# Hybrid retention/convolution/MoE step: late constants, an early root for norm 1, and the first four in-projection blocks taken unit by unit

## The reference, cut to what matters

```python
cond = jax.nn.silu(c)
for l in range(2):
    mod = (cond @ w_mod[l] + b_mod[l])[:, None, :]
    sh1, sc1, gt1, sh2, sc2, gt2 = jnp.split(mod, 6, axis=-1)
    h = rms_norm(x, g_mix_norm[l]) * (1 + sc1) + sh1          # norm 1
    proj = h @ w_in[l]                                        # in-projection, 1024 -> 3072
    q, k, v, g, u, z = split(proj)
    a = u * jax.nn.sigmoid(z)                                 # input of the convolution
    cv, buf_new = causal_depthwise_conv(a, conv_buf[l], w_conv[l], b_conv[l])   # 31 taps
    conv_out = jax.nn.silu(layer_norm(cv, g_conv_ln[l], b_conv_ln[l]))
    ret_out, s_new = retention(rotary(q), rotary(k), v, ...)  # gated by silu(g)
    x = x + gt1 * (concat(ret_out, conv_out) @ w_out[l])
    h = rms_norm(x, g_ffn_norm[l]) * (1 + sc2) + sh2
    x = x + gt2 * grouped_moe(h, ...)                         # 16 experts, 2 per token
return rms_norm(x, g_final), states
```

## Time and profile before

| | |
|---|---|
| median of three runs | 1478.28 us (1475.58 to 1479.06) |
| profiled execution | 1475.93 us, of which the span is 1473.4 us |
| PE busy | 1387.0 us, 94% of the span |
| DVE busy | 671.1 us, 46% |
| ACT busy | 240.4 us, 16% |
| DMA, mean | 341 GB/s |
| chain that ended last | PE 63%, SP's queue 25%, DMA 5%, DVE 3% |

### The profile page before, as it was taken

One profiled execution on the slowest core, in us unless ns is written; L12 is line 12 of the kernel. 1 busy time (PEld: TensorE's weight loads), 2 busy tenths in 40 slices (PEclk: granted clock), 3 DMA queues, 4 the chain that ended last, 5 costly groups with the idle time before them and its releaser, 6 DMA issues.

```text
span 1473.4 us, 20499 instructions
## 1 busy us (share of the span) xinstructions
PE 1387.0 (94%) x7451; PEld 657.1 (45%) x7452; DVE 671.1 (46%) x1955; ACT 240.4 (16%) x398; POOL 93.0 (6%) x143
## 2 busy tenths in 40 slices
PE   5899998999999999999989999889999999999996
PEld 2677663433433333343337766543343333334333
DVE  1598655334333333433326967653343323233343
ACT  1211312111110111111121113311111101111112
POOL 1072010000000000000000710000000000000000
PEclk9799997999999999999999999989999999999999
DMA  9934679999999983999998446799999999899993
GB/s 333 370 115 146 236 263 348 406 410 409 410 410 410 409 310 159 391 410 410 410 409 314 180 144 237 267 374 410 410 409 410 409 410 410 335 389 410 410 409 122
DMA packets 131315, 502.10 MB, mean 341 GB/s; under 512 B 8636, under 2 KB 8956, under 8 KB 131139
## 3 DMA queue, kind: packets, MB, share of 16 engines
q1 hardware_dynamic: 127056, 487.84, 83.8%
q0 software_dynamic: 3600, 11.21, 2.7%
q10 hardware_dynamic: 626, 2.62, 0.6%
HBM read 495.48 MB, written 7.00 MB: 341 GB/s over the span
## 4 chain that ended last, share of the span: by engine, by line
PE 63%; SPq 25%; DMA 5%; DVE 3%; issue 2%; ACT 1%; PEldq 0%; PEld 0%; DVEq 0%; ACTq 0%
PE ps L399 59%; SPq L367 22%; PE ps L402 4%; DMA ring<-in_w_mod 3%; DMA ring<-in_w_exp_up 2%; SPq L379 1%; SPq L322 1%; ACT arena L857 1%; DVE stat L1049 1%; ACT L857 0%; SPq L370 0%; DVE rt L1317 0%; ACT stat L857 0%; SPq L366 0%; SPq L313 0%
## 5 line engine op out<-in xcount | busy, mean ns | idle before, releaser
L399 PE MATMUL ps<-ring,arena 128*64 128x512 f32 x3360 | 755.7, 598 | 21.2 <-DMA ring<-in_w_exp_up 15.2
L399 PEld LDWEIGHTS ps<-ring,arena 128*64 128x64 f32 x3360 | 227.7, 137 | 488.4 <-issue 419.0
L399 PE MATMUL ps<-hT,ring 128*128 128x288 f32 x1024 | 257.9, 413 | 11.9 <-DVE hT L1119 9.6
L857 ACT ACTIVATE arena<-ps 128x512 f32<-128x512 f32 (+3 forms) x238 | 127.7, 551 | 832.5 <-PE ps L399 726.0
L1407 DVE SCALAR_TENSOR_TENSOR xT<-ps,mod,xT 128x256 f32<-128x256 f32 x280 | 132.8, 474 | 256.0 <-PE ps L399 256.0
L399 PEld LDWEIGHTS ps<-hT,ring 128*128 128x128 f32 x1024 | 196.7, 193 | 72.2 <-DVE hT L1119 10.1
L399 PE MATMUL ps<-arena 64*128 64x288 f32 (+4 forms) x1656 | 208.4, 404 | 4.5 <-DVE xT L1460 1.7
L399 PEld LDWEIGHTS ps<-arena 64*128 64x128 f32 (+4 forms) x1656 | 117.6, 159 | 128.5 <-issue 100.0
L1150 DVE SCALAR_TENSOR_TENSOR arena<-arena,wcT 128x256 f32<-128x256 f32 x240 | 123.5, 576 | 1.6
L857 ACT ACT_TABLE_LOAD x49 | 62.9, 1283 | 304.2 <-PE ps L399 300.5
L1441 DVE TENSOR_TENSOR arena<-ps,arena 128x512 f32<-128x512 f32 x35 | 24.2, 691 | 166.7 <-PE ps L399 166.7
(11 more groups left out here) (169 smaller groups left out, 528.0 us busy)
## 6 DMA issues: line engine op xcount, KB each, us to landing
ring<-in_w_exp_gate SPq DMA_DIRECT2D x128, 1024.0 KB, 17.1
ring<-in_w_exp_up SPq DMA_DIRECT2D x128, 1024.0 KB, 18.1
ring<-in_w_exp_down SPq DMA_DIRECT2D x128, 1024.0 KB, 18.1
ring<-in_w_mod SPq DMA_DIRECT2D x48, 1024.0 KB, 9.1
ring<-in_w_in SPq DMA_DIRECT2D x24, 1024.0 KB, 21.0
ring<-in_w_out SPq DMA_DIRECT2D x8, 1024.0 KB, 12.7
big<-in_state_ret POOLq DMA_DIRECT2D x4, 512.0 KB, 10.4
arena<-in_state_ret POOLq DMA_DIRECT2D x4, 512.0 KB, 5.2
```

Source lines behind the costliest of these rows:

```text
L399: return nc.tensor.matmul(out, lhsT, rhs, start=start, stop=stop, skip_group_check=True)
L857: return nc.scalar.activation(out, in_, f, **kw)
```

## The change: what it does

1. **Loads.** SP issues the first two modulation units before the small row loads (`row_loads`), then the other six, then the four units of the in-projection's first group, and only then the convolution history of layer 0 (it was POOL's, 480 KB) and the large part of the constants (it was ACT's, 1173.5 KB). POOL waits for unit 3 before it issues the taps (`wcrows`), the router weights and the router bias.
2. **Norm 1's root.** In the setup ACT takes the root right after the squares, ahead of the copies of the two slabs. For layer 1 and the last norm it takes it at the end of the layer before, with a one-column root ahead of it that brings the table in; DVE scales all eight blocks before it looks at slab 1.
3. **In-projection.** Blocks 0 to 3 go unit by unit: for each of the four units the two k blocks of all four blocks. The transposes of the taps (layer 0) and of the history (both layers) come after block 3, and what depends on them moves: ACT copies the history after the second sigmoid, DVE copies the taps after the first `gate_in`, and the wait for the large constants stands at the rotary step.

```diff
@@ SP @@
-            for row, n, src in (...): sp.dma_start(vrows[row:row + n, :, :], ...)
+            def row_loads(): ...
             for j in range(2):
                 for q in range(UQ):
                     ...
                     sp.dma_start(ring[:, s], mod_v[0, q, :, :, (1 - j) * D:(2 - j) * D]).then_inc(loaded[s], 16)
+                    if s == 1:
+                        row_loads()
             conv_load(0, lambda s: 1)
+            sp.dma_start(cbt[0:120, :, :], ...).then_inc(cb_first, 16)
+            sp.dma_start(cst[:, NFIRST:], consts[:, NFIRST:]).then_inc(in_const, 16)
@@ PE @@
                 pe.drain().then_inc(slab_step, 1)
-                if j == 0:
-                    ...  # two transposes of wcrows
                 pe.wait_ge(mod_evac, j + 1)
...
+                pe.wait_ge(V.hs_ready, 1)
+                for q in range(UQ):
+                    s = G_CONV * UQ + q
+                    pe.wait_ge(loaded[s], layer_load(0)(s))
+                    for n in range(4):
+                        for kk in range(UK):
+                            k = q * UK + kk
+                            if n == 0:
+                                pe.wait_ge(V.h_ready, k + 1)
+                            last = mm(ps[:, n, 0:T], ring[:, s, kk, CONV_COLS[n] * P:(CONV_COLS[n] + 1) * P], hT[:, k, :],
+                                      k == 0, k == KC - 1)
+                        if q == UQ - 1:
+                            last.then_inc(V.inproj_done, 1)
+                n = 4
+                if l == 0:
+                    pe.wait_ge(in_wr, 48)
+                    ...  # two transposes of wcrows
+                ...      # eight transposes of cbt, before: ahead of block 0
@@ ACT @@
-            act.dma_start(cst[:, NFIRST:], consts[:, NFIRST:]).then_inc(in_const, 16)
...
                 a(big[:, k, :], xT[:, k, :], ACT.Square).then_inc(x_squared, 1)
+            act.wait_ge(x_summed, 1)
+            root(stat[:, 1, :], 6, D)
             for j in range(2):
                 act.wait_ge(slab_step, 2 * j + 1)
                 a(modS[:, j, :], ps[:, j, :]).then_inc(mod_evac, 1)
...
-                act.wait_ge(x_summed, l + 1)
-                root(stat[:, 1, :], 6, D)
                 act.wait_ge(V.sh_ready, 1)
                 shifted(M_SH1, V.h_scaled, V.h_ready)
...
+                a(rt[:, 15, 47:48], C("eps"), ACT.Sqrt)
+                act.wait_ge(x_summed, l + 2)
+                root(stat[:, 1, :], 6, D)
                 if l < L - 1:
                     evac_next(1)
...
-            a(stat[:, 1, :], ps[:, 6, 0:T], ACT.Sqrt, scale=1.0 / D, bias=C("eps")).then_inc(fin_rs, 1)
@@ DVE @@
                 for k in range(KC):
-                    if k == 2:
-                        ...  # add_turned(3, 0), hs_ready
                     v.scalar_tensor_tensor(hT[:, k, 0:SEQ], ...).then_inc(V.h_scaled, 1)
+                dve.wait_ge(slab_step, 4 * l + 4)
+                add_turned(3, 0).then_inc(V.sh_ready, 1)
+                ...  # hs_ready
...
                 gate_in(0)
+                if l == 0:
+                    dve.wait_ge(rows_trans, 2)
+                    v.tensor_copy(wcT[:, :, :], ...).then_inc(rows_copied, 1)
@@ POOL @@
+            pool.wait_ge(loaded[UQ - 1], 16)
             pool.dma_start(wcrows[0:TAPS * CT, :, :], ...).then_inc(in_wr, 16)
...
-            pool.dma_start(cbt[0:120, :, :], hist_v[0]).then_inc(cb_loaded, 16)
```

More of the change, by code:

```diff
@@ L309, in _, with row_loads @@
             exp_v = [w.rearrange("l e (q k p) c -> (l e) q p k c", q=UQ, p=P) for w in (w_exp_gate, w_exp_up, w_exp_down)]
[L311 to L315, removed]
+            def row_loads():
+                for row, n, src in ((R_GMIX, 8, g_mix_norm), (R_GFFN, 8, g_ffn_norm), (R_BMOD, NMB, b_mod), (R_BCONV, 4, b_conv),
+                                    (R_GCLN, 4, g_conv_ln), (R_BCLN, 4, b_conv_ln), (R_GRET, 4, g_ret_gn)):
+                    sp.dma_start(vrows[row:row + n, :, :], src.rearrange("l (r p) -> r l p", p=P)).then_inc(in_rows, 16)
+                for l in range(L):
+                    sp.dma_start(vrows[R_GFIN:R_GFIN + 8, l, :], g_final.rearrange("(r p) -> r p", p=P)).then_inc(in_rows, 16)
             for j in range(2):
@@ L459, in _, with layer_load @@
                 pe.drain().then_inc(slab_step, 1)
-                if j == 0:
[L461 to L465, removed]
                 pe.wait_ge(mod_evac, j + 1)
                 mod_turn(2 + j, modS[:, j, :]).then_inc(slab_step, 1)
-            pe.wait_ge(in_wr, 48)
             for l in range(L):
                 pe.wait_ge(mix_open, l + 1)
-                pe.wait_ge(cb_loaded, l * 16 + 16)
+                n = 0
+                def layer_load(k):
+                    return lambda s: l * (16 * LOADS[s]) + 16 * (SETUP[s] + k + 1)
+                CONV_COLS = [0, 4, 1, 5, 2, 6, 3, 7]
+                pe.wait_ge(V.hs_ready, 1)
[14 more added lines that the diff above has]
+                    pe.wait_ge(in_wr, 48)
+                    for w in range(L):
+                        last = tr(ps[:, 7, w * P:w * P + TAPS * CT], wcrows[0:TAPS * CT, w, :], TAPS * CT)
+                    last.then_inc(rows_trans, 1)
+                if l == 0:
+                    pe.wait_ge(cb_first, 16)
+                else:
+                    pe.wait_ge(cb_loaded, l * 16)
                 for ct in range(CT):
@@ L478, in _ @@
                     last.then_inc(V.cb_trans, 1)
[L480 to L484, removed]
+                for g, cols in ((G_CONV, CONV_COLS[4:]), (G_QK, range(8)), (G_VG, range(8))):
                     for m in cols:
[L486 to L492, removed]
-                        for k in range(KC):
[L494 to L498, removed]
+                        if n - 4 >= 8:
+                            pe.wait_ge(V.proj_copied, n - 4 - 8 + 1)
+                        elif n % 2 == 0:
+                            pe.wait_ge(V.a_ready, (n - 4) // 2 + 1)
+                        else:
+                            pe.wait_ge(V.z_sig, (n - 4) // 2 + 1)
+                        for k in range(KC):
+                            if g != G_CONV and m == cols[0] and k % UK == 0:
                                 s = g * UQ + k // UK
@@ L903, in _ @@
                     a(zsig[:, i % 2, :], ps[:, (2 * i + 1) % 4, 0:T], ACT.Sigmoid).then_inc(V.z_sig, 1)
+                    if i == 1:
+                        act.wait_ge(V.pad_ready, 1)
+                        for ct in range(CT):
+                            act.wait_ge(V.cb_trans, ct // 2 * 2 + 2)
+                            a(fullv[:, ct, FRING:].rearrange("p (b w) -> p b w", b=B)[:, :, 0:HIST],
+                              ps[:, 4 + ct // 2, (ct % 2) * 240:(ct % 2) * 240 + 240].rearrange("p (b w) -> p b w", b=B)) \
+                                .then_inc(V.cb_copied, 1)
                 for n in range(16):
@@ L1156, in _ @@
                 gate_in(0)
+                if l == 0:
+                    dve.wait_ge(rows_trans, 2)
+                    v.tensor_copy(wcT[:, :, :], ps[:, 7, 0:L * P].rearrange("p (l r) -> p l r", l=L)[:, :, 0:TAPS * CT]).then_inc(rows_copied, 1)
+                    dve.wait_ge(rows_copied, 2)
                 for tap in FIRST[0]:
@@ L1173, in _ @@
                 dve.wait_ge(V.proj_copied, 8)
+                if l == 0:
+                    dve.wait_ge(in_const, 16)
                 for c in range(2):
```

25 lines of the change are left out of this document (7 added, 18 removed).

## The result

The changed kernel takes 1458.82 us (median of four runs, 1457.57 to 1460.62), the kernel before beside it 1476.93 us (1473.65 to 1479.06): a ratio of 0.988 (95% interval 0.9856 to 0.9904). Forecast were 1460.8 us in 1453 to 1469. The profiled execution of the changed kernel took 1459.87 us, 16.1 less than that of before; its span is 1457.9 us, 15.5 less. A second profile of it comes with the experiments (1463.73 us, span 1460.1).

A forecast was written before the change was run, and what follows sets the result against it. PE (63% of the span) and the weight queue (30%) were taken to bound the kernel. Layer 0's 12.8, layer 1's 3.4 and the last norm's 1.3 sum to 17.5 us off 1478.28: 1460.8 us, range 1453 to 1469.

The forecast's parts named there:

- x's arrival: Layer 0's start: x lands 2.1 us later than 9.44, from a range of 0 to 5.1, behind two queued units.
- the estimate of 3.4 us: Layer 0's start: x's delay if DMA engines alternate packets between queues; in-projection start 37.2, gain below 1.3 us smaller.
- PE's own chain: Layer 0's start: from x's arrival through both slabs, turns and shift to the in-projection takes 24.3 us, so start at 35.9.
- the checkpoint: Start of the convolution layer norm's sum on PE; in layer 0 forecast at 118.1 against 130.86, 12.8 us won.
- E: End of in-projection block 3, 15.5 us after the in-projection's start at full clock; forecast 51.4 in layer 0.
- Full clock in layer 0: Layer 0 from the in-projection: both slabs have their units, so the 3.0 us lost to half clock before disappear.
- 2.75 us of clock loss: Layer 1, block 0 to the layer norm's sum: slabs still paced by DMA, so the low-clock loss of before stays.
- Last norm: Last norm: the one-column root moves the table load into ACT's wait of 2.13 us; 1.3 us won.
- A: Rival, slow start: x or unit 7 late and clock 0.50 at block 0; 8 to 12 us won, 1466 to 1470; chance 0.23.
- B: Rival, everything early: x hardly later, full clock in layer 1 too; up to 2.1 + 2.75 us more, 1456 to 1458; chance 0.20.
- C: Rival, given back: expert weights set the end, only the last norm's 1.3 us stay, 1477; chance 0.04.
- D: Rival, slower: history, constants and state loads delay q and k units for block 8; landing at 90 gives 1482; chance 0.03.

The follow-up runs named there:

- the yardstick: The changed kernel itself, unaltered, measured once more beside the last three experiment kernels: 1461.31 us, ratio 0.9894 against the kernel before.

## Why the prediction was right, and where it was not

The time was right within 2 us, but part of that was luck, because misses of opposite sign met: layer 0 won 9.3 us, not 12.8, layer 1 won 5.8, not 3.4, and 2.0 us were lost over layer 1's experts, where none was forecast.

- *x's arrival: the step that failed most.* Taken were 2.1 us; measured were 4.8 (14.24 against 9.44), nearly the whole 5.1 that stood at the end of the range. Two stretches show why. By x's landing the DMA had moved 298 GB/s x 14.2 us = 4.2 MB in the changed kernel, 231 x 9.4 = 2.2 MB before:

```profile
0.00:14.20 14.20, 1.02 (x8) 0.93 (x9) 1.49 (x2) 2.58 (x3) 0.20 (x4) 1.00 0.87 298
```

```profile
0.00:9.40 9.40, 0.99 (x8) 0.93 (x9) 1.48 (x2) 2.58 (x3) 3.91 (x8) 1.00 0.79 231
```

  So 2.06 MB more went by ahead of x, which is two whole units (2.1 MB). ACT's queue, with x, carried 1.42 MB in all, so some 2.8 of the 4.2 MB were SP's. The queues' own rows say when: by 8 us SP's queue had moved 1.8 MB and ACT's 0.28; in 8 to 11 us the two shared evenly by packets (ACT's is q10, SP's q1; packets, then MB):

```profile
q10 hardware_dynamic: 203, 0.83, 71.9%
q1 hardware_dynamic: 200, 0.35, 30.9%
```

  The Trainium skill has the engines go round the queues packet by packet ("DMA: Bandwidth & Descriptors", Queues, rings and completion order), from which the estimate of 3.4 us came. The trace agrees in 8 to 11 us (203 and 200 packets) and not over the whole (482 and 937).

  Putting x first brought its start back to 9.87 and the in-projection to 35.89. That this is the 35.9 of the prediction is a coincidence: there the start came 26.0 us behind x, and unit 7 set it, not PE's chain of 24.3.
- *PE's own chain, x + 24.3 us.* Measured: 39.47 - 14.24 = 25.2. Slab, copy, turn and shift are as worked out (3.64, 0.77, 0.66, 1.27); what is over is the sum of squares, 6.74 us for 16 records, where before it took 5.45. That group is uneven from run to run: 6.04 us in the second profile, 5.14 to 6.25 in the other kernels.
- *Blocks 0 to 3 and the checkpoint: right.* E = 39.47 + 15.5 = 55.0, and E + 66.7 = 121.7 against 121.56, with DVE last as predicted. That the unit order is what lets the earlier start count is shown in layer 1: block by block 9.6 us are lost there, 3.6 with POOL's state loads out of the way. In layer 0 the two block-by-block runs differ: no wait for a unit in the one, 2.94 us of it in the other.
- *Full clock in layer 0: right in one profile* (1.00 in 20 to 50 us), wrong in the other of the same kernel (17.45 us for the four blocks). Taking it for certain left out a term of 1.7 us that comes and goes. DVE's being last costs 0.9 us at the sum, as worked out (E + 66.7 against 65.7); the lower clock behind it came in one profile of the two.
- *Layer 1: the start was right, the clock not.* From the last unit to the in-projection 4.3 us were won (4.4 forecast). The 2.75 us of clock loss that I kept are gone in both profiles of the changed kernel: E + 65.5 holds without them, 762.08 + 15.5 + 65.5 = 843.1 against 843.07. Before, 4.77 us of idling were followed by a clock of 0.73; now PE idles 1.28 us and the clock is 1.00:

```profile
775.40:785.00 9.60, 9.55 (x29) 7.21 (x30) 2.37 (x7) 5.11 (x12) 2.33 (x3) 0.73 1.02 389
```

```profile
762.00:777.80 15.80, 15.72 (x66) 12.34 (x67) 1.35 (x5) 4.42 (x9) 2.33 (x3) 1.00 1.02 386
```

- *Last norm:* 1.3 us forecast, 1.3 measured from the start of the sum to the root (5.5 us before, 4.2 now), 1.8 to the end of the span.
- *The rivals.* Of A, the late x came, and the low clock in one profile of the two; of B, the full clock in layer 1. C is out: of the 2.0 us lost over layer 1's experts, 1.7 are a lower clock. D is out: no wait for the q and k units stands in the timeline.

The parts are not a sum. Taken from the ratios, at 1475.4 us: the whole change wins 15.6 to 17.7 us; without the early root it loses 3, so that root is worth some 19 to 21; without the unit order 5.9 are left, so that is worth 10 to 12; with the loads as they were (part 1 undone) 10.3, so part 1 is worth 5 to 7. Together that is at least 33, so the parts lean on each other: without the root the other two win nothing. No run has one part alone.

What stays open: why ACT's queue got so little before 8 us, and what decides whether the clock falls behind a short pause. That the gain in the medians (18.1) is larger than in the profiled pair (15.5) is within what medians of so few runs do: beside the yardstick it was 14.1. The half-clock stretches fall differently from run to run elsewhere too (around 224 us, 6.8 us of it in one profile of the changed kernel and 17.1 in the other).

## What to carry to other kernels

When the first load that everything needs shares the DMA with a bulk stream, charge it with all the bytes issued before it, and try it at the head of the bulk queue. Edits at one start are links of one chain: ask for each what it is worth when the others are absent. And look at the granted clock behind each wait of PE, in more than one profile of the same kernel: a lower clock seen once behind a pause is not yet the price of that pause.

## What the runs showed of the hardware

- *A granted clock of 1.00 does not always mean that pace.* In the changed kernel the sum of squares takes 6.74 us from 21.47 (0.42 us for each of 16 records) and, with the same shapes in the second layer, 4.05 us from 750.48 (0.25 us). Both stretches show 1.00, and PE was busy throughout:

```profile
21.50:26.80 5.30, 5.30 (x13) 3.75 (x12) 1.44 (x3) 1.73 (x2) 0.87 (x2) 1.00 1.05 344
750.40:754.60 4.20, 4.20 (x23) 3.08 (x25) 2.01 (x9) 2.40 (x5) 0.00 (x0) 1.00 1.02 406
```

  At the start of a program the pace of the matmuls must be read beside the column. What slows them there no run shows.
- *The same short pause can leave the clock up or down.* Seven profiles have the early root and the unit order, so 14 starts of an in-projection behind a pause of 1.27 or 1.28 us. In eight the four blocks took 15.8 to 16.0 us, in six 17.35 to 18.33. Behind pauses of 4.77 to 9.30 us (before and the late root, both layers) the granted clock was 0.50 each time.
- *Small loads cost a large stream.* With x first, moving POOL's three small loads (196 KB, 0.5 us at 409 GB/s) behind unit 7 made the in-projection start 1.8 us earlier (35.89 to 34.06). In 22 to 30 us SP's queue moved 2.36 MB beside them and 3.28 MB without them, an estimated 2.2 us at 410 GB/s:

```profile
q1 hardware_dynamic: 620, 2.36, 92.1%
q1 hardware_dynamic: 854, 3.28, 102.6%
```
